# Eight of the sixteen input projections of a linear-attention layer as three fp32r products of split operands

## The chip, the cores and the metric

The kernel runs on one core of one Trainium2 chip. The metric is the device time of one execution in microseconds (us), the median of several. Four engines compute, each with an instruction queue of its own that runs in program order: TensorE (PE; its weight loads are shown apart as PEld), VectorE (DVE), ScalarE (ACT) and GpSimd (POOL). SyncE (SP) issues most transfers from memory to the on-chip buffers. Engines wait for one another by semaphores that count up.

## The reference, cut to what matters

The program is a two-layer decoder trunk over 256 tokens of width 1024. The change touches only the start of layer 0, the gated DeltaNet:

```python
def gated_deltanet(h, w_in, conv_w, a_log, dt_bias, g_onorm, w_out):
    proj = h @ w_in                                   # 1024 -> 3072 (q, k, v) + 1024 (z) + 16
    qkv = jax.nn.silu(causal_depthwise_conv(proj[..., :QKV_W], conv_w))
    z = proj[..., QKV_W:QKV_W + V_W].reshape(b_, s_, LA_HEADS, LA_DV)
    ...
    o = chunk_gated_delta_rule(q, k, v, g, beta)      # a triangular solve for each chunk and head
    o = rms_norm(o, g_onorm) * jax.nn.silu(z.astype(jnp.float32))
    return o.reshape(b_, s_, V_W).astype(h.dtype) @ w_out
```

After it come a dense SwiGLU of width 3584, sliding-window attention and a top-2-of-8 expert SwiGLU. All of it is float32.

## The kernel before

**Projections.** `w_in` comes in eight units of 512 columns (2 MB each; `IN_COLS` gives their order), and each unit serves two projections, so there are sixteen, `project(0)` to `project(15)` (lines 622 to 635). One projection gives 256 columns for all 256 tokens: for two blocks `q` of 128 columns it adds up eight matmuls (`k`) with a 128x128 piece of the weights held in the array and `HNT[:, k, :]`, the normed and transposed input, streamed in 256 columns. That is sixteen fp32 matmuls (line 634); the profile shows each as two MATMUL records. When done it adds 1 to `proj_mm`. Projections 0 to 11 are q, k and v: DVE runs the causal convolution on each (`conv(f)`, lines 1611 and 1618) and ACT the silu (line 1258). Projections 12 to 15 are z: ACT takes each out of PSUM with a silu into `ZT` (`z_out`, line 1262).

**The solve.** The triangular solve doubles its block size in levels `lv` = 1 to 6. On PE a level is: `turn` of the level before (16 transposes, line 578), four groups of four matmuls `y` (line 729), four groups `z` (line 739), some small group (values, or the q-k products of line 674), and then `project(6 + lv)`, which fills PE's time. Group g of `y` is copied out by ACT (line 1298, `y_ready`) before group g of `z` may start. DVE's `level(lv)` subtracts each `z` group (line 1699, `u_ready`) and masks the next operand (line 1702). PE has only two PSUM banks for `z`: group 2 waits for DVE's subtraction of group 0, and group 3 for that of group 1. The next `turn` waits for all subtractions. DVE's queue holds `level(lv)`, then small work, then `conv` of the projection that came in this level, then the next level's `level`.

**After the levels.** PE goes through the norms of q, `yv`, `w`, `ks` (lines 756 to 775), `project(13)`, `o` and `vn` (780 to 788), `project(14)`, four transposes for each half (578), `project(15)`, the last `o` (807, 808) and then `w_out` (line 813), 32 matmuls of 512 columns against the two units of `a_w_out`. It waits for both of these units ahead of the first one. `w_out` feeds the residual sum, the second norm, and the dense SwiGLU.

**The split form in use.** The dense layer and the experts already use split operands. ACT copies half a unit to the type fp32r (`dense_high`, line 1338: the high part), DVE subtracts this from the original, in place and again as fp32r (`dense_low`, line 1800), and PE makes three fp32r matmuls for one fp32 product: low weights with high rows, high weights with low rows, high weights with high rows (lines 875 to 877; the rows are split by lines 1345 and 1816).

**Weight slots and SP's order.** A ring of seven slots of 2 MB holds the weights. Units 0 to 9 (eight of `w_in`, two of `a_w_out`) use slots 0 to 2 in turn (`FRONT = 3`), and unit n waits until unit n - 3 is used up. So the first `a_w_out` unit waits for 12 projections and the second for 14; SP's next loads, of the dense weights, wait for `proj_mm` 16, `ks_mm`, `vn_mm`, `o_mm` and `wo_mm`. SP issues in this order only, so a waiting load holds back all that follow. Slots 3 to 6 are in use by the solve until then.

Of the kernel before, what the change touches and what calls it, by code (L numbers as in the profile page):

```python
# [20 lines left out]
ALU = mybir.AluOpType  # L21
# [31 lines left out]
U_IN, U_OUT, U_FF = 0, 8, 10  # L53
IN_COLS = [2, 3, 4, 5, 0, 1, 6, 7]
N_Z = 12
FRONT = 3
RING = [1, 5, 4, 3, 6, 2, 0]
FILLS = [("p", f) for f in range(4, 13)] + [("s", 0), ("p", 13), ("p", 14), ("p", 15)]
U_KV = U_FF + 3 * NSL
# [3 lines left out]

def slot_of(n):

    return n % FRONT if n < U_FF else RING[(n - U_FF) % SLOTS]


def uses(n):

    if n < U_FF:
        return n // FRONT + 1
    return len(range(slot_of(n), U_FF, FRONT)) * (slot_of(n) < FRONT) + (n - U_FF) // SLOTS + 1


def fill_bank(kind, n):
# [87 lines left out]
def build(nc, x, a_norm, a_w_in, a_conv, a_log_decay, a_dt_bias, a_out_norm, a_w_out, kv_norm, kv_w,  # L164
# [6 lines left out]
    with ExitStack() as ctx:  # L171
# [52 lines left out]
        def as_kt(ap):  # L224
            return ap.rearrange("p (k t) -> p k t", t=S)
# [1 line left out]
        HNT = as_kt(hnT[:, :])  # L227
        HS = hs[:, :].rearrange("p (t d) -> p t d", d=D)
        CONV = cbuf[:, :, :].rearrange("p b (m t) -> p (b m) t", t=S)
        ZT = as_kt(zbuf[:, :])  # L230
        R = [as_units(ring[:, 3 + i // 2, 4 * (i % 2):4 * (i % 2) + 4, :].rearrange("p k f -> p (k f)"))
             for i in range(8)]
        X = [as_units(xbuf[:, i, :]) for i in range(4)]
# [10 lines left out]
        def sm(a, n):  # L244
            return small[:, a:a + n]


        DXH = as_kt(bufs_r[ZBUF_R][:, :])
        DXL = as_kt(bufs_r[HNT_R][:, :])
        DHT = [bufs_r[XBUF_R + b][:, :].rearrange("p (z i t) -> p z i t", z=2, i=4) for b in range(2)]  # L250
        DSG, DPR = (xbuf[:, 3, i * 4 * S:(i + 1) * 4 * S].rearrange("p (b t) -> p b t", b=4) for i in range(2))
        DHB = [bufs_r[i][:, :] for i in (CBUF_R, CBUF_R + 1, CBUF_R + 2, HS_R)]

        KVW = SW_KV * HD
        RBW = xbuf[0:N_BUCKETS + 1, 2, 0:SW_HEADS]
# [59 lines left out]
        ba_ready, gate_v, gate_a, cum_ready, gb_ready, egb_ready, dt_ready = (  # L315
            sem(n) for n in ("ba_ready", "gate_v", "gate_a", "cum_ready", "gb_ready", "egb_ready", "dt_ready"))
        proj_mm, conv_done, silu_done, z_done = (sem(n) for n in ("proj_mm", "conv_done", "silu_done", "z_done"))
        tok_tp, tok_a, tok_v, gram_mm, m_ready, t0_scaled = (
            sem(n) for n in ("tok_tp", "tok_a", "tok_v", "gram_mm", "m_ready", "t0_scaled"))
        vt_tp, vt_ready, gq_mm, attn_ready, qe_ready, sq_ready, qn_mm, qn_ready = (  # L320
# [112 lines left out]
        def high_at(j):  # L433

            return 6 * j + 9 if j < NSL - 2 else (HALVES - 4 if j == NSL - 2 else HALVES)

        def load(eng, kind, src, s):
            dst = slot_r(s) if kind == "r" else slot_c(s)
            eng.dma_start(dst, src).then_inc(slot_full[s], 16)
# [4 lines left out]
        @block.sync  # L444
        def _(sp):
            units = static_units()
            sp.dma_start(h[:, :, :], x[0].rearrange("(t p) d -> p t d", p=P)).then_inc(x_in, 16)
            sp.dma_start(cst[:, :], c_main).then_inc(cst_in, 16)

            sp.dma_start(rows1, a_conv[0].rearrange("j (m p) -> (j m) p", p=P)).then_inc(par_in, 16)  # L450
            for r0, r1, src in ((0, KT, a_norm), (GA_FF0, GA_FF0 + 2 * KT, ffn_norm)):
                sp.dma_start(rows2[r0:r1, :], src.rearrange("l (m p) -> (l m) p", p=P)).then_inc(par_in, 16)
            for r0, src in ((GA_KV, kv_norm), (GA_B, b_norm[0])):
                sp.dma_start(rows2[r0:r0 + KT, :], src.rearrange("(m p) -> m p", p=P)).then_inc(par_in, 16)
            for n, (kind, src) in enumerate(units):
                if n == 1:
                    for c0, row in ((0, a_dt_bias), (8, a_log_decay), (16, b_sinks)):
                        sp.dma_start(bcv[:, c0:c0 + row.shape[1]], row[0].partition_broadcast(P)).then_inc(ba_in, 16)
                    sp.dma_start(wba, a_w_in[0].rearrange("(k p) f -> p k f", p=P)[:, :, QKV + D:QKV + D + 16]
                                 ).then_inc(ba_in, 16)  # L460
                i = n - U_FF
                if FRONT <= n < U_FF:
                    sp.wait_ge(*released(n - FRONT))
                elif i == 0:
                    sp.wait_ge(proj_mm, 16)
                elif i == 1:
                    sp.wait_ge(ks_mm, 2)
                elif i == 2:
                    sp.wait_ge(vn_mm, 2)
                elif i in (3, 4):  # L470
                    sp.wait_ge(o_mm, 4)
                elif i in (5, 6):
                    sp.wait_ge(wo_mm, 4)
                elif i >= SLOTS:
                    sp.wait_ge(*released(n - SLOTS))
                load(sp, kind, src, slot_of(n))

            def expert_item(item, e, first):
                for u, (kind, j) in enumerate(moe_sequence()):
                    n = U_MOE + u  # L480
                    if u < SLOTS and first:
                        sp.wait_ge(*released(n - SLOTS))
                    else:
                        sp.wait_ge(m_used, HALVES * item + 2 * (u - SLOTS + 1))
                    load(sp, "r" if kind == "down" else "c", moe_src(kind, j, e), slot_of(n))

            expert_item(0, 0, True)
            with sp.Fori(1, EXPERTS) as e:
                expert_item(e, e, False)
            sp.wait_ge(flag_ready, 1)  # L490
            more = sp.value_load(flag[0:1, 0:1], min_val=0, max_val=S)
            with sp.If(more > WIN):
                with sp.Fori(1, NWIN) as w:
                    with sp.Fori(0, EXPERTS) as e:
                        expert_item(w * EXPERTS + e, e, False)
                sp.wait_ge(m_h, TT * 2 * ITEMS)

            for n in range(2):
                sp.wait_ge(m_h, TT * 2 * EXPERTS - TT * (1 - n))
                c = slice(n * FS, (n + 1) * FS)  # L500
                sp.dma_start(out[0].rearrange("(t p) d -> p t d", p=P)[:, :, c], h[:, :, c]).then_inc(stored, 16)
            sp.wait_ge(stored, 32)
# [73 lines left out]
        def _(pe):  # L576
# [45 lines left out]
            def project(f):  # L622

                u = f // 2
                if f % 2 == 0:
                    landed(pe, U_IN + u)
                b = f
                if f >= 4:
                    fill_free("p", f)
                    b = fill_bank("p", f)  # L630
                for q in range(2):
                    c0 = (2 * (f % 2) + q) * P
                    for k in range(KT):
                        m = pe.matmul(bk[b][:, q * S:(q + 1) * S], slot_c(slot_of(u))[:, k, c0:c0 + P],  # L634
                                      HNT[:, k, :], start=k == 0, stop=k == KT - 1)
                m.then_inc(proj_mm, 1)

            def key_tokens(g):
# [574 lines left out]
        def _(act):  # L1213
# [65 lines left out]
            def turned(lv):  # L1279
                for g in range(4):  # L1280
                    act.wait_ge(t_tp, 4 * lv + g + 1)
                    act.activation(R[4][:, quads(g), :], as_quad(g), ACT.Copy).then_inc(t_ready, 1)

            for f in range(3):
                silu(f)
            act.wait_ge(gate_a, 2)
# [5 lines left out]
            silu(4)  # L1292
            turned(0)
            silu(5)
            for lv in range(1, NLEV):
                for g in range(4):
                    act.wait_ge(y_mm, 4 * (lv - 1) + g + 1)
                    act.activation(X[3][:, quads(g), :], as_quad(g), ACT.Copy).then_inc(y_ready, 1)
                if lv < NLEV - 1:
                    turned(lv)  # L1300
                if lv == 1:
                    silu(6)
                if lv <= 5:
                    silu(6 + lv)
            act.wait_ge(silu_done, 12)
            for b in range(4):
                act.activation(SQ_Q[:, 2 * b:2 * b + 2, :], CONV[:, 2 * b:2 * b + 2, :], ACT.Square
                               ).then_inc(sq_ready, 1)
            z_out(12)
            act.wait_ge(qn_mm, 1)  # L1310
            for half in range(2):
                act.wait_ge(yv_mm, half + 1)
                act.activation(HSU[:, quads(2 * half), :], as_quad(2 * half), ACT.Copy).then_inc(yv_ready, 1)
            for half in range(2):
                act.wait_ge(w_mm, half + 1)
                act.activation(R[6][:, quads(2 * half), :], as_quad(4 + half), ACT.Copy, scale=-1.0
                               ).then_inc(w_ready, 1)
            z_out(13)
            for half in range(2):
                act.wait_ge(o_mm, half + 1)  # L1320
                act.activation(X[3][:, quads(2 * half), :], as_quad(2 * half), ACT.Square).then_inc(o_sq, 1)
# [209 lines left out]
        def _(dve):  # L1531
# [181 lines left out]
            def attn(g):  # L1713
                dve.wait_ge(gq_mm, g + 1)
                dve.tensor_tensor(R[0][:, quads(g), :], as_quad(2 + g % 2), X[2][:, quads(g), :], ALU.mult
                                  ).then_inc(attn_ready, 1)

            solve_in(0)
            conv(4)
            solve_in(1)  # L1720
# [1 line left out]
            level(1)  # L1722
            conv(6)
            conv(7)
            level(2)
            then(dve.tensor_tensor(kt, cs[:, 0:HEADS], sm(176, HEADS), ALU.mult))
            conv(8)
            level(3)
            dve.wait_ge(pow_out, powers[0])
            for g in range(2):  # L1730
                values(g)
            conv(9)
            mask(0)
            mask(1)
            level(4)
            for g in range(2, 4):
                values(g)
            conv(10)
            mask(2)
            mask(3)  # L1740
            level(5)
            for g in range(2):
                attn(g)
            conv(11)
            for half in range(2):
                gs = quads(2 * half)
                last = dve.tensor_tensor(R[5][:, gs, :], R[5][:, gs, :], bc(kt[:, 4 * half:4 * half + 4], P), ALU.mult)
            last.then_inc(t0_scaled, 1)
            level(6)
            for g in range(2, 4):  # L1750
                attn(g)
            dve.wait_ge(silu_done, 12)
            dve.wait_ge(egb_ready, 2)
            for half in range(2):
# [5 lines left out]
            for half in range(2):  # L1760
                dve.wait_ge(ks_mm, half + 1)
                dve.tensor_copy(STATE[:, 4 * half:4 * half + 4, :], as_quad(1 + 2 * half)).then_inc(st_ready, 1)
            dve.wait_ge(qn_ready, 1)

            def normed(t):

# [431 lines left out]
```

## Time and profile before

| | |
|---|---|
| median of 3 runs | 1608.07 us (1606.32 to 1609.74) |
| the profiled execution | 1604.6 us, span 1602.7 us |
| PE busy | 1566.6 us, 98% |
| DVE busy | 1173.9 us, 73% |
| ACT busy | 895.4 us, 56% |
| first projection starts | 15.92 us |
| last `w_out` matmul ends | 250.27 us |
| dense layer starts on PE | 260.21 us |

The trace's times count from the span's start. A row of the timeline gives start, duration, engine, line and operation, and in square brackets how long the engine stood idle ahead of it and what it then got. A matmul's duration contains the time in the array behind its last column, so that successive ones overlap; how fast they follow one another is read from their starts. In the chain of waits that time is taken out: there a row's duration is what it adds to the end.

### The profile page before, as it was taken

The page shows a single profiled execution, that of the slowest core. Times are in us where ns is not written, and L with a number is a line of the kernel's source. Part 1 is how long each engine was busy: PE and PEld are TensorE (multiplying, and loading weights), DVE is VectorE, ACT ScalarE, POOL GpSimd, SP SyncE. Part 2 cuts the span into 40 slices and gives each one's busy share as a digit, 9 for nine tenths or more (in the row PEclk, how much of TensorE's full clock was granted, in tenths as well). Part 3 has the DMA queues.
Part 4 walks back from the last instruction along what each step waited for, and adds up shares of the span by engine and source line. Part 5 has one row for each costly group of instructions (what it writes and reads, how often), then busy time and mean ns, then how long its engine had stood idle before and what let it go on. Part 6 is the DMA issues. An engine that isn't in the chain of part 4 may idle for free.

```text
span 1602.7 us, 20486 instructions
## 1 busy us (share of the span) xinstructions
PE 1566.6 (98%) x8062; PEld 1308.9 (82%) x8062; DVE 1173.9 (73%) x1106; ACT 895.4 (56%) x836; POOL 50.6 (3%) x43
## 2 busy tenths in 40 slices
PE   7999998999999998999999999999999999999998
PEld 6899976999996566888888888888888888888886
DVE  3956234544444565988988988988988989989885
ACT  1332222433442353777777677677677677767763
POOL 1000010000001100000000000000000000000000
PEclk9999998999999998999999999999999999999999
DMA  6311166454546315999999999999999999999990
GB/s 235 132 54 53 57 244 230 167 194 174 199 170 211 105 53 219 376 379 344 377 381 343 377 381 348 370 379 363 358 380 366 344 384 371 351 380 367 353 365 28
DMA packets 184958, 439.30 MB, mean 274 GB/s; under 512 B 5325, under 2 KB 5477, under 8 KB 184896
## 3 DMA queue, kind: packets, MB, share of 16 engines
q1 hardware_dynamic: 182528, 430.52, 73.3%
q0 software_dynamic: 2368, 7.91, 1.4%
q8 instruction: 44, 0.72, 0.2%
q14 instruction: 18, 0.15, 0.0%
HBM read 436.29 MB, written 2.65 MB: 274 GB/s over the span
## 4 chain that ended last, share of the span: by engine, by line
PE 97%; DVE 1%; ACT 1%; DMA 0%; issue 0%; POOL 0%; DVEq 0%; ACTq 0%; POOLq 0%
PE bank L1167 13%; PE bank L1169 13%; PE bank L1168 13%; PE bank L634 7%; PE bank L1154 6%; PE bank L1152 6%; PE bank L1153 6%; PE bank L578 4%; PE bank L875 3%; PE bank L876 3%; PE bank L877 3%; PE bank L1000 2%; PE bank L813 2%; PE bank L917 2%; PE bank L739 1%; PE bank L861 1%
## 5 line engine op out<-in xcount | busy, mean ns | idle before, releaser
L1987 DVE TENSOR_TENSOR ring_r<-ring,buf_r 128x2048 fp32r<-128x2048 f32 x336 | 751.1, 2284 | 29.3 <-ACT buf_r L1448 29.3
L1448 ACT ACTIVATE buf_r<-ring 128x2048 fp32r<-128x2048 f32 x336 | 629.6, 1915 | 52.2 <-PE bank L1154 43.4
L1167 PE MATMUL bank<-ring_r,buf_r 128*128 128x512 f32 x896 | 354.9, 396 | 1.6 <-DVE buf_r L2100 1.6
L1169 PE MATMUL bank<-buf_r,buf_r 128*128 128x512 f32 x896 | 349.7, 390 | 0.0
L1168 PE MATMUL bank<-buf_r,buf_r 128*128 128x512 f32 x896 | 349.0, 390 | 0.0
L1169 PEld LDWEIGHTS bank<-buf_r,buf_r 128*128 128x128 f32 x896 | 168.2, 188 | 36.0
L1167 PEld LDWEIGHTS bank<-ring_r,buf_r 128*128 128x128 f32 x896 | 168.4, 188 | 34.7 <-DVE buf_r L2100 1.7
L1168 PEld LDWEIGHTS bank<-buf_r,buf_r 128*128 128x128 f32 x896 | 168.5, 188 | 33.4
L1152 PE MATMUL bank<-ring_r,buf_r 128*128 128x512 f32 x448 | 175.9, 393 | 0.0
L1154 PE MATMUL bank<-buf_r,buf_r 128*128 128x512 f32 x448 | 174.6, 390 | 0.0
L1153 PE MATMUL bank<-buf_r,buf_r 128*128 128x512 f32 x448 | 174.3, 389 | 0.0
L1800 DVE TENSOR_TENSOR ring_r<-ring,buf_r 128x2048 fp32r<-128x2048 f32 x42 | 96.1, 2291 | 102.9 <-ACT buf_r L1338 102.9
L1338 ACT ACTIVATE buf_r<-ring 128x2048 fp32r<-128x2048 f32 x42 | 80.4, 1918 | 112.6 <-PE bank L877 82.2
L1472 ACT ACTIVATE buf_r<-bank 128x512 fp32r<-128x512 f32 x56 | 33.5, 599 | 183.7 <-PE bank L578 170.6
L875 PE MATMUL bank<-buf_r,ring_r 128*128 128x256 f32 x448 | 128.2, 286 | 3.4 <-DVE buf_r L1816 2.4
L876 PE MATMUL bank<-buf_r,buf_r 128*128 128x256 f32 x448 | 127.9, 286 | 0.0
L877 PE MATMUL bank<-buf_r,buf_r 128*128 128x256 f32 x448 | 127.8, 285 | 0.0
L634 PE MATMUL bank<-hnT,ring 128*128 128x256 f32 x512 | 115.3, 384 | 1.3 <-ACT hnT L1227 1.3
L634 PEld LDWEIGHTS bank<-hnT,ring 128*128 128x128 f32 x512 | 97.7, 193 | 15.2 <-ACT hnT L1227 1.7
L1154 PEld LDWEIGHTS bank<-buf_r,buf_r 128*128 128x128 f32 x448 | 84.1, 188 | 17.8
L1153 PEld LDWEIGHTS bank<-buf_r,buf_r 128*128 128x128 f32 x448 | 84.2, 188 | 17.1
L1152 PEld LDWEIGHTS bank<-ring_r,buf_r 128*128 128x128 f32 x448 | 84.1, 188 | 17.0
(285 smaller groups left out, 1622.9 us busy)
## 6 DMA issues: line engine op xcount, KB each, us to landing
ring<-in_moe_w_gate SPq DMA_DIRECT2D x56, 2048.0 KB, 8.0
ring<-in_moe_w_up SPq DMA_DIRECT2D x56, 2048.0 KB, 8.1
ring<-in_moe_w_down SPq DMA_DIRECT2D x56, 2048.0 KB, 8.0
ring<-in_a_w_in SPq DMA_DIRECT2D x8, 2048.0 KB, 9.4
ring<-in_dense_w_gate SPq DMA_DIRECT2D x7, 2048.0 KB, 8.9
ring<-in_dense_w_up SPq DMA_DIRECT2D x7, 2048.0 KB, 9.1
ring<-in_dense_w_down SPq DMA_DIRECT2D x7, 2048.0 KB, 7.8
ring<-in_a_w_out SPq DMA_DIRECT2D x2, 2048.0 KB, 9.3
```

Of the source, the lines that this page charges most:

```text
L634: m = pe.matmul(bk[b][:, q * S:(q + 1) * S], slot_c(slot_of(u))[:, k, c0:c0 + P], HNT[:, k, :], start=k == 0, stop=k == KT - 1)
L875: pe.matmul(o, low[:, c], DXH[:, k, :], start=k == 0, stop=False)
L876: pe.matmul(o, high[:, c], DXL[:, k, :], start=False, stop=False)
L877: ins = pe.matmul(o, high[:, c], DXH[:, k, :], start=False, stop=k == KT - 1)
L1152: pe.matmul(o, hh, low[:, c], start=j == 0 and i == 0, stop=False)
L1153: pe.matmul(o, hl, high[:, c], start=False, stop=False)
L1154: ins = pe.matmul(o, hh, high[:, c], start=False, stop=j == NSL - 1 and i == 3)
L1167: pe.matmul(o, xh, low[:, c], start=k == 0, stop=False)
L1168: pe.matmul(o, xl, high[:, c], start=False, stop=False)
L1169: ins = pe.matmul(o, xh, high[:, c], start=False, stop=k == KT - 1)
L1448: act.activation(HB[m % NHB], half_words(m, U_MOE), ACT.Copy).then_inc(m_wh, 1)
L1987: dve.tensor_tensor(half_low(m, U_MOE), half_words(m, U_MOE), HB[m % NHB], ALU.subtract).then_inc(m_wl, 1)
```

## The change

- Projections 8 to 15 become three fp32r products for each fp32 one (`SPLIT = 8`): 48 fp32r matmuls of 256 columns instead of 16 fp32 ones.
- ACT gets four operations that make the high part of the rows (`PXH`, in the old place of z), ahead of the copies of level 1, and one `proj_high(f)` for each of the eight projections: in levels 1 to 6 behind the `y` copies, and behind `z_out(12)` and `z_out(13)`. It waits for the weights of its unit and, from f = 10 on, for the projection two before, since there are two buffers of high parts (`PWH`).
- DVE gets four subtractions for the low part of the rows (`PXL`, over `HNT`), ahead of `level(2)`, and one `proj_low(f)` for each of the eight: 8 ahead of `level(2)`, 9 to 12 each behind a `conv`, 13 behind `level(6)`, 14 behind the last `attn`, 15 ahead of the output norm. Each waits for its `proj_high`.
- PE waits at each split projection for its `proj_low`, and at projection 8 for the low rows.
- The two buffers of high parts lie in weight slot 2. So only slots 0 and 1 are left for the input weights (`FRONT = 2`): unit n waits for unit n - 2. `a_w_out` goes to slots 0 and 2: its first unit waits for 14 projections (before: 12), its second for all 16 (before: 14).
- `ZT`, and in the dense layer `DXH` and one of the four buffers of `DHB`, trade places; there is no further instruction for that.

```diff
-FRONT = 3
+FRONT = 2
+SPLIT = 8
...
-    return n % FRONT if n < U_FF else RING[(n - U_FF) % SLOTS]
+    return (n % FRONT if n < U_OUT else 2 * (n - U_OUT)) if n < U_FF else RING[(n - U_FF) % SLOTS]
...
-                if FRONT <= n < U_FF:
+                if n == U_OUT + 1:
+                    sp.wait_ge(proj_mm, 16)
+                elif FRONT <= n < U_FF:
                     sp.wait_ge(*released(n - FRONT))
...
+                if f == SPLIT:
+                    pe.wait_ge(px_low, 4)
+                if f >= SPLIT:
+                    pe.wait_ge(p_wl, f - SPLIT + 1)
...
+                        low, high = (w[:, k, q * P:(q + 1) * P] for w in (low_half(f), PWH[f % 2]))
+                        pe.matmul(o, low, PXH[:, k, :], start=k == 0, stop=False)
+                        pe.matmul(o, high, PXL[:, k, :], start=False, stop=False)
+                        m = pe.matmul(o, high, PXH[:, k, :], start=False, stop=k == KT - 1)
...
+            def proj_high(f):
+
+                if f % 2 == 0:
+                    landed(act, U_IN + f // 2)
+                if f >= SPLIT + 2:
+                    act.wait_ge(proj_mm, f - 1)
+                act.activation(PWH[f % 2], raw_half(f), ACT.Copy).then_inc(p_wh, 1)
...
             silu(5)
+            act.wait_ge(hn_ready, 4)
+            for b in range(4):
+                act.activation(PXH[:, 2 * b:2 * b + 2, :], HNT[:, 2 * b:2 * b + 2, :], ACT.Copy).then_inc(px_high, 1)
             for lv in range(1, NLEV):
                 for g in range(4):
                     act.wait_ge(y_mm, 4 * (lv - 1) + g + 1)
                     act.activation(X[3][:, quads(g), :], as_quad(g), ACT.Copy).then_inc(y_ready, 1)
+                proj_high(7 + lv)
                 if lv < NLEV - 1:
                     turned(lv)
...
+            def proj_low(f):
+
+                dve.wait_ge(p_wh, f - SPLIT + 1)
+                dve.tensor_tensor(low_half(f), raw_half(f), PWH[f % 2], ALU.subtract).then_inc(p_wl, 1)
...
             conv(7)
+            for b in range(4):
+                dve.wait_ge(px_high, b + 1)
+                kk = slice(2 * b, 2 * b + 2)
+                dve.tensor_tensor(PXL[:, kk, :], HNT[:, kk, :], PXH[:, kk, :], ALU.subtract).then_inc(px_low, 1)
+            proj_low(8)
             level(2)
             then(dve.tensor_tensor(kt, cs[:, 0:HEADS], sm(176, HEADS), ALU.mult))
             conv(8)
+            proj_low(9)
             level(3)
...
             conv(9)
+            proj_low(10)
             mask(0)
             mask(1)
             level(4)
```

DVE's queue ahead of `level(2)` before the change: the convolution of projection 7 (lines 1611 and 1618), then the level's subtractions and masks.

```order
L1611 TENSOR_SCALAR cbuf<-bank,cw 128x256 x2
L1618 SCALAR_TENSOR_TENSOR cbuf<-bank,cw,cbuf 128x255 x2
L1618 SCALAR_TENSOR_TENSOR cbuf<-bank,cw,cbuf 128x254 x2
L1618 SCALAR_TENSOR_TENSOR cbuf<-bank,cw,cbuf 128x253 x2
L1699 TENSOR_TENSOR ring<-ring,bank 128x512
L1702 TENSOR_TENSOR xbuf<-ring 128x512
```

The same place in the changed kernel; line 1768 makes the low rows and line 1756 is `proj_low(8)`.

```order
L1646 TENSOR_SCALAR cbuf<-bank,cw 128x256 x2
L1653 SCALAR_TENSOR_TENSOR cbuf<-bank,cw,cbuf 128x255 x2
L1653 SCALAR_TENSOR_TENSOR cbuf<-bank,cw,cbuf 128x254 x2
L1653 SCALAR_TENSOR_TENSOR cbuf<-bank,cw,cbuf 128x253 x2
L1768 TENSOR_TENSOR buf_r_57<-hnT,buf_r_61 128x512 x4
L1756 TENSOR_TENSOR ring_r_49<-ring,ring_r_51 128x8x256
L1734 TENSOR_TENSOR ring<-ring,bank 128x512
L1737 TENSOR_TENSOR xbuf<-ring 128x512
```

Five instructions now stand between the convolution and the level's first subtraction.

SP's queue of loads before the change, with what each waits for (from the second `w_in` unit on):

```order
L439 DMA ring<-in_a_w_in 128x8x512 x2
L439 DMA ring<-in_a_w_in 128x8x512 [waits proj_mm] x5
L439 DMA ring<-in_a_w_out 128x8x512 [waits proj_mm] x2
L439 DMA ring<-in_dense_w_gate 128x8x512 [waits proj_mm]
L439 DMA ring<-in_dense_w_up 128x8x512 [waits ks_mm]
```

And in the changed kernel:

```order
L447 DMA ring<-in_a_w_in 128x8x512
L447 DMA ring<-in_a_w_in 128x8x512 [waits proj_mm] x6
L447 DMA ring<-in_a_w_out 128x8x512 [waits proj_mm] x2
L447 DMA ring<-in_dense_w_gate 128x8x512 [waits proj_mm]
L447 DMA ring<-in_dense_w_up 128x8x512 [waits ks_mm]
```

One `w_in` load has moved from the unconditional ones to those that wait; the counts for which the `a_w_out` loads wait have risen by two each, so that the second now waits for the same count as the first dense load.

## Rows read from the trace of the kernel before

**Rows 1.** Page, chain of work that ended last, shares of the span by engine:

```profile
PE 97%; DVE 1%; ACT 1%; DMA 0%; issue 0%; POOL 0%; DVEq 0%; ACTq 0%; POOLq 0%
```

**Rows 2.** That chain in order of time; start us, us, what:

```profile
84.68 2.90 PE bank L739 x24
...
101.00 2.90 PE bank L739 x24
...
103.97 1.13 PE bank L739 x8
105.10 6.91 PE bank L634 x32
...
169.96 3.79 PE bank L739 x32
...
210.55 0.87 PE bank L578 x8
...
218.34 0.22 PE bank L807 x2
...
221.91 10.30 PE bank L813 x24
```

**Rows 3.** Timeline of PE: the first projection, and fp32r matmuls in the dense layer:

```profile
15.92 9.22 PE L634 MATMUL bank<-hnT,ring 128*128 128x256 f32 x32 [1.30 <-ACT hnT L1227]
...
266.00 0.28 PE L875 MATMUL bank<-buf_r,ring_r 128*128 128x256 f32 x1
...
280.03 0.28 PE L875 MATMUL bank<-buf_r,ring_r 128*128 128x256 f32 x1
```

**Rows 4.** Page, costliest groups: busy us, mean ns of one, idle before:

```profile
L1800 DVE TENSOR_TENSOR ring_r<-ring,buf_r 128x2048 fp32r<-128x2048 f32 x42 | 96.1, 2291 | 102.9 <-ACT buf_r L1338 102.9
L1338 ACT ACTIVATE buf_r<-ring 128x2048 fp32r<-128x2048 f32 x42 | 80.4, 1918 | 112.6 <-PE bank L877 82.2
```

**Rows 5.** Timeline of DVE from level 2 to the dense layer:

```profile
96.63 2.68 DVE L1618 SCALAR_TENSOR_TENSOR cbuf<-bank,cw,cbuf 128x255 f32<-128x255 f32 x6
101.93 0.69 DVE L1699 TENSOR_TENSOR ring<-ring,bank 128x512 f32<-128x512 f32 x1 [2.62 <-PE bank L739]
...
118.26 0.69 DVE L1699 TENSOR_TENSOR ring<-ring,bank 128x512 f32<-128x512 f32 x1 [2.55 <-PE bank L739]
...
132.75 1.41 DVE L1711 TENSOR_TENSOR xbuf<-xbuf,cst 128x512 f32<-128x512 f32 x2
135.52 0.69 DVE L1699 TENSOR_TENSOR ring<-ring,bank 128x512 f32<-128x512 f32 x1 [1.36 <-PE bank L739]
...
170.89 0.69 DVE L1699 TENSOR_TENSOR ring<-ring,bank 128x512 f32<-128x512 f32 x1 [1.42 <-PE bank L739]
...
203.58 1.29 DVE L1779 TENSOR_TENSOR xbuf<-bank,small 128x512 f32<-128x512 f32 x2
...
259.37 2.50 DVE L1816 TENSOR_TENSOR buf_r<-hnT,buf_r 128x512 fp32r<-128x512 f32 x4 [1.51 <-ACT buf_r L1345]
```

**Rows 6.** Timeline of ACT in level 1 and behind the projections:

```profile
81.76 0.65 ACT L1258 ACTIVATE cbuf<-cbuf 128x512 f32<-128x512 f32 x1
82.28 1.25 ACT L1298 ACTIVATE xbuf<-bank 128x512 f32<-128x512 f32 x2
...
226.29 3.71 ACT L1338 ACTIVATE buf_r<-ring 128x2048 fp32r<-128x2048 f32 x2 [3.75 <-DMA ring<-in_dense_w_gate]
...
258.71 2.19 ACT L1345 ACTIVATE buf_r<-hnT 128x512 fp32r<-128x512 f32 x4
```

**Rows 7.** Timeline of SP: the first dense load:

```profile
218.37 0.37 SPq L439 DMA_DIRECT2D ring<-in_dense_w_gate  x1
```

**Rows 8.** Page, DMA issues: KB each, median us to landing:

```profile
ring<-in_a_w_out SPq DMA_DIRECT2D x2, 2048.0 KB, 9.3
```

**Rows 9.** Stretches: us, engines' busy time, then granted clock, DMA share, GB/s:

```profile
250.30:254.00 3.70, 0.00 (x0) 0.00 (x0) 2.72 (x5) 0.00 (x0) 1.40 (x2) 1.00 0.68 210
254.00:256.00 2.00, 1.17 (x9) 1.17 (x10) 1.25 (x4) 0.00 (x0) 0.23 (x1) 0.90 1.05 407
```

More of the change, by code:

```diff
@@ L64, in slot_of @@
 def slot_of(n):
-    return n % FRONT if n < U_FF else RING[(n - U_FF) % SLOTS]
+    return (n % FRONT if n < U_OUT else 2 * (n - U_OUT)) if n < U_FF else RING[(n - U_FF) % SLOTS]
 def uses(n):
-    if n < U_FF:
-        return n // FRONT + 1
-    return len(range(slot_of(n), U_FF, FRONT)) * (slot_of(n) < FRONT) + (n - U_FF) // SLOTS + 1
+    return sum(slot_of(m) == slot_of(n) for m in range(n + 1))
 def fill_bank(kind, n):
@@ L229, in build @@
         CONV = cbuf[:, :, :].rearrange("p b (m t) -> p (b m) t", t=S)
-        ZT = as_kt(zbuf[:, :])
+        ZT = as_kt(cbuf[:, 2, :])
+        PXH, PXL = as_kt(bufs_r[ZBUF_R][:, :]), as_kt(bufs_r[HNT_R][:, :])
+        PWH = [ring_r[2][:, i * BS:(i + 1) * BS].rearrange("p (k c) -> p k c", k=KT) for i in range(2)]
         R = [as_units(ring[:, 3 + i // 2, 4 * (i % 2):4 * (i % 2) + 4, :].rearrange("p k f -> p (k f)"))
@@ L245, in sm @@
             return small[:, a:a + n]
-        DXH = as_kt(bufs_r[ZBUF_R][:, :])
+        DXH = as_kt(bufs_r[CBUF_R + 2][:, :])
         DXL = as_kt(bufs_r[HNT_R][:, :])
@@ L251, in build @@
         DSG, DPR = (xbuf[:, 3, i * 4 * S:(i + 1) * 4 * S].rearrange("p (b t) -> p b t", b=4) for i in range(2))
-        DHB = [bufs_r[i][:, :] for i in (CBUF_R, CBUF_R + 1, CBUF_R + 2, HS_R)]
+        DHB = [bufs_r[i][:, :] for i in (CBUF_R, CBUF_R + 1, ZBUF_R, HS_R)]
         KVW = SW_KV * HD
@@ L317, in build @@
         proj_mm, conv_done, silu_done, z_done = (sem(n) for n in ("proj_mm", "conv_done", "silu_done", "z_done"))
+        px_high, px_low, p_wh, p_wl = (sem(n) for n in ("px_high", "px_low", "p_wh", "p_wl"))
         tok_tp, tok_a, tok_v, gram_mm, m_ready, t0_scaled = (
@@ L435, in high_at, with raw_half, low_half @@
             return 6 * j + 9 if j < NSL - 2 else (HALVES - 4 if j == NSL - 2 else HALVES)
+        def raw_half(f):
+            return slot_c(slot_of(f // 2))[:, :, (f % 2) * S:(f % 2 + 1) * S]
+        def low_half(f):
+            return ring_r[slot_of(f // 2)].rearrange("p (k c) -> p k c", k=KT)[:, :, (f % 2) * S:(f % 2 + 1) * S]
         def load(eng, kind, src, s):
@@ L630, in project @@
                     b = fill_bank("p", f)
+                if f == SPLIT:
+                    pe.wait_ge(px_low, 4)
+                if f >= SPLIT:
+                    pe.wait_ge(p_wl, f - SPLIT + 1)
                 for q in range(2):
                     c0 = (2 * (f % 2) + q) * P
+                    o = bk[b][:, q * S:(q + 1) * S]
                     for k in range(KT):
-                        m = pe.matmul(bk[b][:, q * S:(q + 1) * S], slot_c(slot_of(u))[:, k, c0:c0 + P],
-                                      HNT[:, k, :], start=k == 0, stop=k == KT - 1)
+                        if f < SPLIT:
+                            m = pe.matmul(o, slot_c(slot_of(u))[:, k, c0:c0 + P], HNT[:, k, :], start=k == 0,
+                                          stop=k == KT - 1)
+                            continue
+                        low, high = (w[:, k, q * P:(q + 1) * P] for w in (low_half(f), PWH[f % 2]))
+                        pe.matmul(o, low, PXH[:, k, :], start=k == 0, stop=False)
+                        pe.matmul(o, high, PXL[:, k, :], start=False, stop=False)
+                        m = pe.matmul(o, high, PXH[:, k, :], start=False, stop=k == KT - 1)
                 m.then_inc(proj_mm, 1)
@@ L1309, in _ @@
             z_out(12)
+            proj_high(14)
             act.wait_ge(qn_mm, 1)
@@ L1318, in _ @@
             z_out(13)
+            proj_high(15)
             for half in range(2):
@@ L1738, in _ @@
             conv(10)
+            proj_low(11)
             mask(2)
@@ L1744, in _ @@
             conv(11)
+            proj_low(12)
             for half in range(2):
@@ L1749, in _ @@
             level(6)
+            proj_low(13)
             for g in range(2, 4):
                 attn(g)
+            proj_low(14)
             dve.wait_ge(silu_done, 12)
@@ L1763, in _ @@
             dve.wait_ge(qn_ready, 1)
+            proj_low(15)
             def normed(t):
```

## Prediction

> **What bounds the kernel now.** I read the page's chain of waits first: 97% of the span is PE [rows 1]. Then the same chain in order of time. From 15.92 us, when the first projection starts, to the last `w_out` matmul at 250.27 it holds PE rows alone, with gaps of 0.07 us at most, so in this whole stage a microsecond taken off PE is a microsecond off the end, as long as nothing else then comes late. In that chain a projection costs 6.91 us [rows 2]. The second thing to see is how little room the levels leave. Four groups of `z` should take 16 matmuls at the rate of the first three groups, 2.90 / 12 x 16 = 3.9 us at most; in level 2 the last group starts only at 103.97, 0.07 us after the third group's end at 103.90 [rows 2]. It waits there for DVE's second subtraction, so DVE has no slack at all in this place: if DVE's level starts later by d, PE's `z` ends later by d. The third is DVE's idle time just ahead of each level, which is what the change can put work into for nothing. The fourth is the tail: which transfer does `w_out` wait for, and how long does one take.
>
> **PE's gain.** In the dense layer the same three fp32r products of 256 columns run at full clock: from 266.00 to 280.03 us there are 117 steps [rows 3], 0.120 us each. A split projection is 2 x 8 x 3 = 48 such matmuls, 48 x 0.120 = 5.76 us, against 6.91 [rows 2]. Eight of them: 8 x 1.15 = **9.2 us less**.
>
> The Trainium skill ("TensorE: Matmul & The Clock Gate", Back-to-back issue gap) gives a smaller step at full clock, the column count over 2.4 GHz plus 2.5 ns, an estimate of 0.109 us here and of 5.2 us a projection; the same section says that weight loads in a real stream raise it. The trace has the step of exactly this form, and I take the trace's.
>
> **ACT's row split, level 1.** Four copies to fp32r took 2.19 us [rows 6]. They stand behind `silu(5)` and ahead of the `y` copies, the first of which starts at 82.28 [rows 6]. So that one starts at 84.47 and ends about 0.6 us later (1.25 us for two), 85.08; PE wants it at 84.68 [rows 2]. Everything behind in the level moves by **0.4 us**. The eight `proj_high` (1.92 us each [rows 4]) come behind the `y` copies, when ACT has nothing to do until PE is through `z` and a projection; those after `z_out(12)` and `z_out(13)` likewise. Nothing.
>
> **DVE's new work, ahead of the levels.** A `proj_low` is 2.29 us [rows 4], the row split 2.50 us [rows 5]. Each is set against DVE's idle time ahead of the level:
> - Level 2: 2.50 + 2.29 = 4.79 us in a gap of 2.62 (convolution's end 99.31 to 101.93) [rows 5]: late by **2.2 us**.
> - Level 3: 2.29 in a gap of 2.55 [rows 5]: nothing, with 0.26 us to spare.
> - Level 4: 2.29 in a gap of 1.36 [rows 5]: late by **0.9**. Level 5 has the same gap and work: **0.9**.
> - Level 6: `proj_low(12)` and the scaling in a gap of 1.42 [rows 5]: late by 0.87. Here `z` took 3.79 us whole [rows 2] without waiting for DVE, so a part is absorbed; the third group waits for the first subtraction, some **0.6**.
>
> The projection that follows each level (now 5.76 us) covers the rest of DVE's level, so the lateness does not pile up. Sum with level 1: 0.4 + 2.2 + 0.9 + 0.9 + 0.6 = **5.0 us back**.
>
> **After the levels.** `proj_low(13)` lies beside projection 12. `proj_high(15)` and `proj_low(15)` put 1.9 + 2.3 us ahead of the output norm, whose results were ready at 204.87 [rows 5], while PE takes them only after projection 14, at 210.55 [rows 2]; with that projection 1.15 us shorter there is about 1 us left. Nothing, but thin.
>
> **Input weights with two slots.** A load waits for the projection two units back and lands some 9.3 us later [rows 8], the same size. In the levels a unit lasts two levels of some 17 us; the tightest is unit 3, released by projection 3 and wanted two projections and two small stages later, 19 us on. Nothing.
>
> **The second unit of `a_w_out`.** It was released by projection 14, it is now released by the last one. PE ends that at 218.34 and starts `w_out` at 221.91, 3.57 us later [rows 2]. The nearest row is the first dense load, released by the same count: issued at 218.37 [rows 7], landed at 226.29, when ACT stops waiting for it [rows 6], 7.95 us after the projection's end, with other loads issued right behind it. The new load takes its place as the first of them. PE stalls 7.95 - 3.57 = **4.4 us**. With the page's 9.3 us for `a_w_out` [rows 8] it would be 5.8. The dense loads behind it land one load later, but the dense layer starts 42 us after the projections' end, and DVE's splits of them would still be over before `w_out` ends. Nothing more.
>
> **Sum.** -9.2 + 5.0 + 4.4 = +0.2 us. The profiled execution took 1604.6 us and becomes 1604.8; it lies 3.5 us under the median, and the same 0.2 us on the median gives **1608.3 us**. What follows the dense layer's start is not touched and only shifts. About 0.2%, 3.2 us, is what a measurement of this kernel can tell from no change.
>
> **The rivals.**
> A. *The clock falls in the new stall.* A few us without a matmul stand ahead of `w_out`. After `w_out`'s end at 250.27 the clock was still full up to 254 and fell before 256 [rows 9], so a pause of 4.4 us is just about short of that; one of 5.8 is not. Coming back costs what the first projection paid, 9.22 - 6.91 = 2.3 us [rows 2, 3]. From the forecast: +2.5, 1610.6; with the late landing of 5.8 us it is +3.9, 1612.0, slower by more than can be missed. The point from which it decides is a pause of some 5 us. For it: nothing else runs on PE there. Against it: the nearest landing is the short one.
> The Trainium skill's page on TensorE (Why this matters for your kernels) warns of just this, idle gaps between bursts that send the clock back to its lower level; by that rule rival A is likelier than the rows alone say.
> B. *DVE's lateness is swallowed.* If `z` groups or the levels have room that I don't see (a record's start is not its wait), the 5.0 us shrink to about 1 and the result is -3.8, 1604.3. Against it: the last `z` group starts right upon DVE's second subtraction in each of levels 1 to 5.
> C. *A split projection runs at the pace of fp32's passes.* An fp32 projection is 64 passes of 256 columns in 6.91 us, 0.108 each; 48 of these are 5.18 us, the gain 13.8 and the result -4.4, 1603.7. Against it: the 117 steps at 0.120 [rows 3]. The skill's formula, told above, would come out at nearly this.
> D. *The split products cost more here*: a half-empty pipeline at each switch between fp32 and fp32r and at each wait for `p_wl`, or high parts that come late to DVE. Half a microsecond on each of eight projections is +4: 1612.3. Nothing in the trace shows such a switch in mid-stream.
>
> **How the numbers follow.** The forecast with both ends of its unknown terms (stall 4.4 to 5.8, level 6 between 0 and 0.87, thin covers) spans -0.5 to +2, 1607.5 to 1610: chance 0.45. A: 0.25, of which 0.15 lands within 0.2% and 0.10 beyond. B: 0.10, half of it beyond 3.2 us. C: 0.05. D: 0.15, most of it beyond. Faster 0.12, same 0.63, slower 0.25. The range takes in B's and C's times and A's and D's upper ones: 1603.8 to 1612.6.
>
> **What would show it.** In the new trace: a split projection of 5.7 to 5.8 us from its first matmul to the next line's (C: 5.2; D: over 6.2). DVE's idle time ahead of levels 2, 4, 5 and 6 gone, and `z` of level 2 at about 6.1 us instead of 4.1, of levels 4 and 5 at about 5 (B: as before). PE idle for 4.4 us ahead of the first `w_out` matmul, ended by the load of `a_w_out`; the granted clock at 1.0 in it (A: 0.5, and the first `w_out` group of 24 records well over 10.30 us). The stretch from 15.92 us to `w_out`'s end is 234.35 us now and should be 234.6. The forecast is wrong above all if the load lands much earlier or later than 8 us after the last projection, or if a level waits for something that had room before.

## The result and the profile after

The changed kernel takes 1610.08 us (median of 17 runs) against 1605.95 for the kernel before (17 runs beside them): ratio 1.0023, 95% interval 1.0013 to 1.0033, so some 3.7 us slower. The forecast was 1608.3 us, +0.2 us, with 1603.8 to 1612.6 as the range. The time lies inside, 1.8 us above the forecast. The difference between the two kernels was forecast 3.5 us too low, and that is beyond the noise: the interval of the ratio, 2.1 to 5.3 us, begins above +0.2. The time came out nearer than the difference because the forecast started from 1608.07 us, a median of three runs that lies 2.1 us above this one of 17.

The profiled execution shows less than that: 1606.12 us against 1604.6, span 1604.3 against 1602.7. Its chain of waits in order of time says why (start us, us, what), beside [rows 2]:

```profile
15.95 7.17 PE bank L650 x32
...
82.47 0.50 ACT xbuf L1330
83.01 3.16 PE bank L760 x24
...
97.91 2.41 DVE buf_r L1768 x4
100.32 2.20 DVE ring_r L1756
102.52 0.61 DVE ring L1734
103.13 0.14 issue
103.26 1.13 PE bank L760 x8
...
147.99 2.20 DVE ring_r L1756
150.19 0.61 DVE xbuf L1746
150.83 0.70 DVE xbuf L1746
151.56 0.70 DVE ring L1734
...
215.60 4.27 issue
219.87 13.43 PE bank L834 x24
```

Where there was PE alone, DVE stands in the chain: the row split (line 1768) and `proj_low` (1756) ahead of the subtraction (1734) for which `z` waits. In front of `w_out` there is a gap of 4.27 us in which no engine is in the chain. Behind it, the first 24 records of `w_out` took 13.43 us, against 10.30 [rows 2]. And the first projection took only 7.17 us, against 9.22 [rows 3], which has nothing to do with the change, since the matmuls are the same and nothing new stands ahead of them. That the clock had risen earlier in this execution is inferred from the pace: from 15.90 to 20.00 us PE shows 19 matmul records here and 10 in the kernel before, though the profile's clock column reads 1.00 for both. Without that 2.05 us the span would be 3.6 us longer than before, close to the measured 3.7. That is partly chance: this execution lies 4.0 us below the median of its 17 runs, the profiled one of the kernel before 1.4 us below its own, and the two traces don't show where the others lose more.

PE's timeline in the changed kernel, the idle time ahead of `z` in levels 1, 2, 4 and 5:

```profile
83.01 4.36 PE L760 MATMUL bank<-ring,xbuf 128*128 128x128 f32 x32 [0.35 <-ACT xbuf L1330]
103.26 2.33 PE L760 MATMUL bank<-ring,xbuf 128*128 128x128 f32 x16 [1.88 <-DVE ring L1734]
135.41 2.33 PE L760 MATMUL bank<-ring,xbuf 128*128 128x128 f32 x16 [0.92 <-DVE ring L1734]
152.39 2.33 PE L760 MATMUL bank<-ring,xbuf 128*128 128x128 f32 x16 [0.92 <-DVE ring L1734]
```

Stretches around the gap (PE busy, PEld, DVE, ACT, POOL, then the granted clock, DMA share and GB/s):

```profile
212.00:215.60 3.60, 3.60 (x33) 3.41 (x31) 2.13 (x3) 1.19 (x2) 0.00 (x0) 1.00 0.63 197
215.60:219.87 4.27, 0.00 (x0) 0.03 (x1) 1.79 (x5) 0.60 (x1) 1.64 (x1) 0.88 1.05 397
219.87:222.00 2.13, 2.13 (x3) 1.10 (x4) 0.53 (x1) 0.00 (x0) 0.00 (x0) 0.50 1.05 386
222.00:226.00 4.00, 4.00 (x6) 1.55 (x6) 0.00 (x0) 0.00 (x0) 0.00 (x0) 0.54 1.06 390
```

The clock was full when PE fell idle and had gone to its lower level, 1.2 GHz, before `w_out` began. In the kernel before it stood at 1.00 through the same place (218 to 226 us).

The whole account up to `w_out`'s last matmul, from the pieces of both chains, in us:

| | forecast | profile |
|---|---|---|
| eight projections, 6.91 to 5.76 each | -9.2 | -9.2 |
| level 1 (ACT's row split) | +0.4 | +0.6 |
| level 2 | +2.2 | +1.9 |
| level 3 | 0 | 0 |
| level 4, level 5 | +0.9, +0.9 | +0.85, +0.87 |
| level 6 | +0.6 | +0.7 |
| wait for the second `a_w_out` unit | +4.4 | +4.3 |
| first 24 records of `w_out`, at the lower clock | 0 | +3.1 |
| first projection, clock up earlier | 0 | -2.05 |
| sum | +0.2 | +1.1 |

(`w_out` ends at 251.35 us, before at 250.27.) A split projection is 5.76 us: projection 8 runs from 105.59 to 111.35.

### The profile page after: what moved, and what is told of

Read it like the earlier page. It is cut to its first block, busy times and chain, and to the rows that moved or that the text cites. A ratio compares the mean times of both kernels' runs of the same rounds, so it can differ in the third digit from the quotient of the medians.

```text
span 1604.3 us, 20768 instructions
## 1 busy us (share of the span) xinstructions
PE 1559.1 (97%) x8190; PEld 1306.1 (81%) x8190; DVE 1193.8 (74%) x1118; ACT 911.3 (57%) x848; POOL 50.6 (3%) x43
## 4 chain that ended last, share of the span: by engine, by line
PE 94%; DVE 3%; ACT 1%; issue 1%; DMA 0%; SPq 0%; POOL 0%; DVEq 0%; ACTq 0%; POOLq 0%
PE bank L1188 13%; PE bank L1190 13%; PE bank L1189 13%; PE bank L1175 6%; PE bank L1173 6%; PE bank L1174 6%; PE bank L650 3%; PE bank L588 3%; PE bank L896 3%; PE bank L898 3%; PE bank L897 3%; PE bank L834 2%; PE bank L1021 2%; PE bank L938 2%; PE bank L882 1%; PE bank L883 1%
## 5 line engine op out<-in xcount | busy, mean ns | idle before, releaser
L1190 PEld LDWEIGHTS bank<-buf_r,buf_r 128*128 128x128 f32 x896 | 168.5, 188 | 36.1
L1189 PEld LDWEIGHTS bank<-buf_r,buf_r 128*128 128x128 f32 x896 | 168.8, 188 | 33.6
L1175 PEld LDWEIGHTS bank<-buf_r,buf_r 128*128 128x128 f32 x448 | 84.1, 188 | 17.8
L1174 PEld LDWEIGHTS bank<-buf_r,buf_r 128*128 128x128 f32 x448 | 84.2, 188 | 17.1
L896 PEld LDWEIGHTS bank<-buf_r,ring_r 128*128 128x128 f32 x448 | 86.0, 192 | 4.2 <-issue 4.0
L897 PEld LDWEIGHTS bank<-buf_r,buf_r 128*128 128x128 f32 x448 | 86.0, 192 | 0.2
```

The lines of the kernel that those rows point to most:

```text
L896: pe.matmul(o, low[:, c], DXH[:, k, :], start=k == 0, stop=False)
L897: pe.matmul(o, high[:, c], DXL[:, k, :], start=False, stop=False)
L1174: pe.matmul(o, hl, high[:, c], start=False, stop=False)
L1175: ins = pe.matmul(o, hh, high[:, c], start=False, stop=j == NSL - 1 and i == 3)
L1189: pe.matmul(o, xl, high[:, c], start=False, stop=False)
L1190: ins = pe.matmul(o, xh, high[:, c], start=False, stop=k == KT - 1)
```

## The experiments

Each was timed beside the kernel before, whose medians there differ somewhat from the one above, so ratios are compared. Where the clock is in question, the mean granted clock over all runs is given too.

**The wait split in two.** Here the first unit of `a_w_out` covers the landing of the second.

```diff
-            for n in range(2):
-                landed(pe, U_OUT + n)
+            landed(pe, U_OUT)
             pe.wait_ge(og_ready, 2)
             w_out(0, 0, range(KT))
+            landed(pe, U_OUT + 1)
             w_out(0, 1, range(4))
```

> The changed kernel with one wait moved: w_out waits for the first a_w_out unit, does its first eight matmuls (6.9 us), and only then waits for the second. Theory S (the late second load costs a stall of 4.3 us and, through the clock that falls in it, 3.1 us more): no PE idle time ahead of w_out, its first 24 records back at about 10.3 us instead of 13.4, and 7.4 us off the changed kernel: 3.7 us under the kernel before. Rival R (the stall costs only its own length; the rest of the measured loss of some 3.7 us comes from elsewhere, such as switching between fp32 and fp32r): 4.3 us off the changed kernel, 0.6 us under the kernel before.

Measured: 1603.88 us against 1606.59, ratio 0.9984 (0.9973 to 0.9995). PE's timeline:

```profile
217.24 10.46 PE L834 MATMUL bank<-ring,hnT 128*128 128x512 f32 x24
```

The idle time is gone, and so are the 3 us behind it. One moved wait takes the change from 0.23% slower to 0.16% faster. The ratios 1.0023 and 0.9984 are 6.3 us apart; 7.4 were expected and 4.3 under the rival, and with intervals of 1.6 and 1.8 us on either side the time alone doesn't decide between them. The profiles do, for their two executions: the 24 records took 10.46 us, not 13.4, and from the end of the first projection to the last `w_out` matmul PE took 220.9 us, against 228.2 in the changed kernel, 7.4 less. For the average execution the clock's share is not shown by this pair. The fall in the changed kernel's profile alone is 6.8 us at the lower level (by the stretches above), but over all runs the mean granted clock is 0.9894 here and 0.9889 there, which is 34.1 and 35.6 us at the lower level (twice the missing share of the span): 1.5 us less. Where the clock falls instead in the other executions, no trace shows.

**The splits in idle time.** `proj_low` stands ahead of the convolutions, where DVE waits for PE anyway, and ACT splits the rows while it waits for the first `turn`.

```diff
             conv(6)
+            proj_low(8)
             conv(7)
...
-            proj_low(8)
             level(2)
             then(dve.tensor_tensor(kt, cs[:, 0:HEADS], sm(176, HEADS), ALU.mult))
-            conv(8)
             proj_low(9)
+            conv(8)
```

and likewise for 10, 11 and 12; on ACT the four row copies move from behind `silu(5)` to behind `silu(4)`.

> The changed kernel with the splitting work moved into idle time: proj_low(8) ahead of conv(7), proj_low(9) to proj_low(12) each ahead of the convolution that they followed, and ACT's split of the rows behind silu(4). The same instructions, the stall ahead of w_out kept. Theory S (DVE's late levels and ACT's row split cost 4.9 us: 0.6, 1.9, 0, 0.85, 0.87, 0.69 in levels 1 to 6): only level 2 keeps some 0.4 us, 4.5 us off the changed kernel, 0.8 us under the kernel before. Rival R (another wait stands right behind DVE's in the levels, so that an early split gives little): less than 1.5 us off, over 2 us above the kernel before.

Measured: 1603.53 us against 1606.59, ratio 0.9982 (0.9972 to 0.9992), so 6.6 us off the changed kernel (intervals of 1.6 us on either side), more than the 4.5 counted. DVE's timeline around level 3 (`proj_low(9)` is line 1756, now in front of the convolution):

```profile
106.80 2.29 DVE L1756 TENSOR_TENSOR ring_r<-ring,ring_r 128x2048 fp32r<-128x2048 f32 x1
110.76 0.88 DVE L1646 TENSOR_SCALAR cbuf<-bank,cw 128x256 f32<-128x256 f32 x2 [1.67 <-PE bank L656]
111.67 2.68 DVE L1653 SCALAR_TENSOR_TENSOR cbuf<-bank,cw,cbuf 128x255 f32<-128x255 f32 x6
116.97 0.69 DVE L1734 TENSOR_TENSOR ring<-ring,bank 128x512 f32<-128x512 f32 x1 [2.62 <-PE bank L760]
```

The subtraction costs nothing there: DVE still waits 1.67 us for the projection behind it, and has its 2.62 us ahead of the level again. Level 3 had cost nothing in the changed kernel either; what was paid shows in level 4, in DVE's wait ahead of its subtraction and in PE's `z`:

```profile
133.09 0.69 DVE L1734 TENSOR_TENSOR ring<-ring,bank 128x512 f32<-128x512 f32 x1 [1.36 <-PE bank L760]
131.92 4.33 PE L760 MATMUL bank<-ring,xbuf 128*128 128x128 f32 x32
```

DVE has its 1.36 us again, and the 32 records of `z` run in one piece, where the changed kernel had 0.92 us of idle time in the middle. Level 2 keeps 0.2 us (its first three groups of `z` take 3.07 us instead of 2.90). Rival B of the prediction, that the lateness is swallowed, is dead: it was paid, and it comes back. The trace of this kernel has no surplus over the count. From the first projection to the last `w_out` matmul it took 233.1 us against 235.4, but the clock's dips lay elsewhere (the second projection 8.69 us instead of 7.00, `yv` and `w` together 1.6 us longer, `w_out`'s first 24 records 12.13 instead of 13.43) and the wait was 0.4 us longer; on equal terms it is 4.8 us shorter.

**Both.**

> Both edits of the two runs beside it. Theory S: the whole gain of eight shorter projections, 9.2 us, less some 0.4 us of level 2, so 8.8 us under the kernel before (ratio 0.9945); from the first projection to the last w_out matmul about 225.5 us at full clock instead of 234.4. Rival R: the gains don't add up, for instance because the dense weights, which now come one load later, are missed sooner: 4 to 6 us under the kernel before.

Measured: 1597.7 us against 1606.59, ratio 0.9941 (0.9925 to 0.9956). From the first projection's start at 16.19 us, the last `w_out` matmul is over at 242.76:

```profile
182.81 2.74 PE bank L790 x16
185.55 1.79 PE bank L796 x16
193.10 1.79 PE bank L801 x16
204.21 0.87 PE bank L588 x8
214.41 10.30 PE bank L834 x24
224.71 0.87 PE bank L588 x8
225.58 17.18 PE bank L834 x40
```

226.6 us against 234.4. The 225.5 that were expected took the kernel before's first projection of 9.22 us and full clock behind it. In this execution the first took 7.17, the second 8.69 instead of 7.00, and `yv` and `w` (lines 785 and 790), partly at the lower clock, 1.6 us more: together +1.3. Without it the stretch is 225.3 us, so the gains add up and rival R is out.

**PE kept busy in the wait.** Four matmuls of 512 columns ahead of `w_out`, whose result is overwritten; they are extra work, and the wait for the load stays.

```diff
+            landed(pe, U_OUT)
             pe.wait_ge(og_ready, 2)
+            for k in range(4):
+                pe.matmul(bk[WO_BANK[0][0]][:, :], HNT[:, k, tok(0)], slot_c(slot_of(U_OUT))[:, k, :],
+                          start=k == 0, stop=k == 3)
+            landed(pe, U_OUT + 1)
             w_out(0, 0, range(KT))
```

> The changed kernel with four more matmuls of 512 columns, 3.4 us, ahead of w_out while the second a_w_out unit is on its way; their result is overwritten, and the wait for the load stays as it was. It tells the stall's own length from the clock's part. Theory S: the granted clock stays at 1.0 from the last projection on, w_out's start doesn't move, its first real 24 records take 10.3 us, 3.1 us off the changed kernel, 0.6 us above the kernel before. Rival R (the clock's fall there is of this one execution, most have none): no change against the changed kernel, 3.7 us above the kernel before.

Measured: 1606.19 us against 1606.59, ratio 0.9995 (0.9983 to 1.0007). PE's timeline and the stretch of the wait:

```profile
220.35 3.60 PE L842 MATMUL bank<-ring,hnT 128*128 128x512 f32 x8
225.00 10.57 PE L834 MATMUL bank<-ring,hnT 128*128 128x512 f32 x24 [1.05 <-DMA ring<-in_a_w_out]
```

```profile
221.00:225.00 4.00, 2.95 (x7) 0.95 (x6) 2.00 (x5) 0.15 (x1) 1.64 (x1) 1.00 1.05 400
225.00:229.00 4.00, 4.00 (x10) 1.85 (x11) 0.32 (x1) 0.00 (x0) 0.00 (x0) 1.00 1.06 388
```

The load lands no earlier (8.0 us after the last projection, 7.8 in the changed kernel), the clock stays at 1.00, and from ratio 1.0023 to 0.9995 it is 4.5 us faster (by the two intervals 2 to 7), where 3.1 were expected. So work that computes nothing makes this kernel faster, and as the wait is as long as before, this gain is the clock's alone. The gain shows in the medians only: the profiled execution had dips in level 2 and behind the norms of q, and at 237.7 us its stretch is no shorter. It is also not an affair of one execution: over all runs the mean granted clock is 0.9889 in the changed kernel and 0.9919 here, which is 35.6 and 25.9 us at the lower level, 9.7 us less, worth half of that, 4.9 us. The kernel before, timed beside it, has 0.9905 (30.4 us). So the filler took away more time at the lower level than the fall in the wait had in the changed kernel's profile (6.8 us); what else it changed is open.

**The late load in the kernel before.** Projections in fp32 and three slots; only the load of the second unit waits as in the changed kernel.

```diff
-                if FRONT <= n < U_FF:
+                if n == U_OUT + 1:
+                    sp.wait_ge(proj_mm, 16)
+                elif FRONT <= n < U_FF:
```

> The kernel before, fp32 projections and three slots, with one edit: the load of the second a_w_out unit waits for all 16 projections, as in the changed kernel. The stall by itself, with no split product near it. Theory S: PE idle some 4.3 us ahead of w_out, the clock falls in it in most executions, w_out's first 24 records take 12 to 13.4 us: 5.5 to 7.4 us above the kernel before. Rival R (only the stall's length counts): 4.3 us above, with w_out's first 24 records at 10.3.

Measured: 1611.3 us against 1606.44, ratio 1.0028 (1.0017 to 1.0040), 4.5 us, with 2.7 to 6.4 as the interval. PE's timeline:

```profile
230.83 11.97 PE L815 MATMUL bank<-ring,hnT 128*128 128x512 f32 x24 [4.43 <-issue]
242.63 1.04 PE L580 MATMUL bank<-cst,xbuf 128*128 128x128 f32 x8
```

The late load alone makes the idle time (4.43 us) and a slow start of `w_out` (11.97 us), with no split product in the kernel. The time by itself fits the rival better than the 5.5 to 7.4 us expected, whose low end is still inside the interval. The profile is of one of the two longest of the twelve executions (1617.4 us) and shows 1.7 us lost to the clock in `w_out`. Over all runs the mean granted clock is 0.9906, and 0.9902 in the kernel before beside it: on average the late load added no time at the lower level. So here the wait's own length accounts for the time, and how often the clock falls in it, or what it gives back elsewhere, stays open.

**The changed kernel once more.**

> The changed kernel once more, unchanged, beside the run above: a further profile tells whether the clock falls in the stall again, and the time how the changed kernel stands on this chip. Theory S: 3 to 4 us above the kernel before, the clock at half within the stall or just behind it, w_out's first 24 records over 11.5 us. Rival R: w_out's first 24 records at 10.3 us, and still 3 to 4 us above.

Measured: 1611.91 us against 1606.44, ratio 1.0022 (1.0006 to 1.0038). PE's timeline:

```profile
220.61 13.09 PE L834 MATMUL bank<-ring,hnT 128*128 128x512 f32 x24 [4.84 <-issue]
```

The clock fell in the wait again, and over these six runs its mean is 0.9890, as in the first measurement (0.9889). Two of the six times are near 1605 us, that of the profile among them, and four near 1612, so their median is a poor figure for the distance.

**Late in levels 4 to 6 only, and the best version again.** The first is the version with both edits, with `proj_low(9)` to `proj_low(12)` back behind their convolutions.

> The version with both edits, but with proj_low(9) to proj_low(12) put back behind their convolutions, so that DVE is late in levels 4, 5 and 6 alone. Theory S (lateness costs its own length): 0.85 + 0.87 + 0.69 = 2.4 us above the version with both edits. Theory C (PE's pauses in the levels also lower its clock in some executions, which is why moving all the splits gave 6 us where 4.5 were counted): 3 us or more above it, with a mean granted clock over its runs that is lower.

> The version with both edits once more, beside the run below, for a firmer time of the best version. As before: 8 to 10 us under the kernel before, w_out's first 24 records at 10.3 us and no PE idle time ahead of them, no idle time of PE ahead of z in the levels.

Measured: 1597.43 us for the version with both edits, ratio 0.9948 (0.9933 to 0.9962), and 1600.14 for the other, 0.9963 (0.9948 to 0.9977). The difference is 2.7 us of medians, between the 2.4 of the one theory and the 3 of the other, and the mean clocks (0.9907 and 0.9904) can't be told apart; with intervals of over 2 us on either side the times don't decide. The two traces do: PE's `z` takes 0.9, 0.9 and 0.7 us longer in levels 4, 5 and 6, so the lateness there costs its own length. In level 4, for one, PE's idle time is back (timeline of the second version):

```profile
134.81 2.33 PE L760 MATMUL bank<-ring,xbuf 128*128 128x128 f32 x16 [0.92 <-DVE ring L1734]
```

If the surplus of the moved splits (6.6 us for 4.5 counted) is one, it must then lie in earlier levels. The place for it is level 2, with the longest pause. It is seen once, in the kernel with the busy wait, where the clock fell in level 2's pause (timeline of PE, and the stretch behind it):

```profile
105.23 3.64 PE L760 MATMUL bank<-ring,xbuf 128*128 128x128 f32 x16 [1.88 <-DVE ring L1737]
```

```profile
105.20:108.90 3.70, 3.67 (x18) 3.70 (x19) 2.97 (x5) 0.00 (x0) 0.00 (x0) 0.54 0.00 0
```

The same sixteen records took 2.33 us in the changed kernel's own profile. One of the four profiles with this pause shows the fall. That it explains the surplus is argued, not shown, and the surplus itself is within the intervals.

## Why the prediction was right or wrong

**The chain.** Right: PE set the pace from the first projection to `w_out`, so each term could be added up along it.

**PE's gain.** Right to a tenth: 5.76 us for a split projection, so nothing is lost at the switches between fp32 and fp32r either; rivals C (5.18 us) and D fall with that row. Here the step in the trace held, and the 0.109 us a matmul estimated from the Trainium skill's formula for an isolated matmul ("TensorE: Matmul & The Clock Gate", Back-to-back issue gap) did not: 48 of those would be 5.2 us. The prediction took from that section that weight loads raise the step; the section says so for small column counts and the contrary for large ones.

**DVE's work ahead of the levels.** Right in method and nearly in size: 4.9 us for 5.0, level by level. Setting each new instruction against the idle time in front of the next step that PE waits for was what it took. The runs add what the prediction didn't look for: there is idle time on the other side of the convolution too. With the subtraction moved there, 1.67 us of it are left in level 3.

**ACT's row split.** 0.6 for 0.4.

**The second unit of `a_w_out`.** Right: 4.27 us for 4.4. The load landed 7.8 us after the last projection, near the 7.95 of the nearest row and not at the 9.3 of the profile's page; in the four other profiles with that wait it took 8.0 to 8.4.

**The clock in the wait.** This is the step that failed. The text put it into rival A, at a chance of 0.25, with the argument that "a pause of 4.4 us is just about short of that": after `w_out`'s end the clock had still been full up to 254 us, 3.7 us on, and it had fallen before 256 [rows 9]. The row says more than was read from it: a mean of 0.90 over 2.00 us is 0.4 us at the lower level, so the clock fell near 255.6, 5.3 us after `w_out`, when PE was already at work again. And one fall says how late the clock fell once, not how early it may: in the changed kernel it fell in both profiles some 3.2 us into the pause, in the late-load kernel 3.9 and in that with the early splits 4.5 us. The price was also low: 2.3 us from the first projection, where the clock, by the pace of the records, rose partway through, against 3.1 and 2.8 in the two profiles. The Trainium skill's page on TensorE (Why this matters for your kernels) warns of idle gaps between bursts of matmuls, and this case's traces agree: the profiles show four idle gaps of 4.27 to 4.84 us ahead of `w_out`, two in the changed kernel, one in the late-load kernel and one in that with the early splits, and behind each `w_out`'s first 24 records took 11.97 to 13.43 us. With rival A at its measured price the forecast difference would have been 0.2 + 3.1 = 3.3 us, against 3.7 measured. That the clock's fall costs the average execution so much is less sure than that it costs these two: the filler gave back 4.5 us, but the split wait and the late load hardly moved the mean clock.

**The chances.** No change within 0.2% was given 0.63 and slower 0.25. The ratio is at the edge, 1.0023, its interval reaches into both. That the time lies in the range says little for the mechanism: the range took in the times of rivals A to D as well.

## What to carry to other kernels

Where a change takes a buffer from a prefetch, find the first consumer of the load that is now late, and check whether it waits for more than it needs: here a wait for two units, of which the first matmuls use one, made the difference between 0.23% slower and 0.16% faster. Price a new pause of TensorE of such a length with the clock's fall in it as the likely case: here all four profiles with one of 4.3 to 4.8 us show it, and filler work in the pause gained 4.5 us. But the late load in the kernel before cost about its own length on average, so the fall is no fixed price. And put helper work where its engine already waits for the bound engine, ahead of the step that is waiting, and not between that step and the next one on the path: the same subtractions made PE late by 4.3 us in one place and by 0.2 in the other. Moving them and the wait made the changed kernel 0.5 to 0.6% faster than the kernel before, where it had been 0.23% slower.

## What the runs showed of the hardware

The clock falls in other places too. In the version with both edits, sixteen matmuls of one column each (line 777, the norms of q; 32 records) kept PE busy in the record, and the clock still went down behind them (stretches as above, the first is that of the sixteen):

```profile
176.70:180.20 3.50, 3.50 (x34) 3.50 (x33) 0.96 (x1) 2.40 (x2) 0.00 (x0) 1.00 0.00 0
180.20:182.80 2.60, 2.60 (x18) 2.60 (x18) 2.60 (x4) 0.60 (x1) 0.00 (x0) 0.71 0.00 0
182.80:185.50 2.70, 2.70 (x18) 2.70 (x17) 0.03 (x1) 1.19 (x2) 0.00 (x0) 0.65 0.00 0
```

The two groups behind them took 2.57 and 2.74 us, against 1.89 and 1.79 in the changed kernel's profile, where the clock stayed at 1.00 in the same place. A busy share of 100% in PE's row is thus no guard against the lower level. Six of the ten profiles of this case have this dip, that of the kernel before with its load made late among them, so it is not the split products' doing. The other four, the kernel before, the changed one twice and the one with the split wait, take 1.89 and 1.79 us there; what decides it is not known.
